# Group norm to the end in one block: memory normed once, its projections ahead of w_o and amid the conformer, norm gates and convolution taps between their tiles

## The reference, cut to what matters

```python
memn = rmsnorm(mem, mem_norm_g)                     # 256 memory tokens, the same in both layers
# layer 0: RWKV time mix. y is the scan's output, bonus and g come from the same inputs
m = jnp.mean(y, axis=-1, keepdims=True)             # over the 64 channels of a head
var = jnp.mean(jnp.square(y - m), axis=-1, keepdims=True)
y = ((y - m) * lax.rsqrt(var + GN_EPS)).reshape(B, T, D) * ln_g + ln_b
out = ((y + bonus) * g) @ w_o                       # g = sigmoid(xg @ g1) @ g2
# layer 1: conformer convolution
u = h @ w_in + b_in
u = u[..., :D] * jax.nn.sigmoid(u[..., D:])
u = causal_dwconv(u, dw) + dw_b                     # 31 taps for each channel
out = jax.nn.silu(layernorm(u, ln_g, ln_b)) @ w_out + b_out
# both layers, after x = x + out
x = x + memory_cross_attention(rmsnorm(x, g_x), memn, w_q, w_kv, w_o)   # kv = memn @ w_kv
x = x + conv_ffn(rmsnorm(x, g_f), w_in, dw3, w_out)
```

## Time and profile before

| | |
|---|---|
| median of 3 runs | 2953.36 us |
| profiled execution, its own time | 2956.45 us |
| its span, first to last instruction | 2954.7 us |
| TensorE (PE) busy | 2668.1 us, 90% |
| VectorE (DVE) busy | 1157.0 us, 39% |
| ScalarE (ACT) busy | 960.7 us, 33% |
| GpSimd (POOL) busy | 1004.0 us, 34% |
| mean granted clock of TensorE | 0.925 of 2.4 GHz |
| DMA moved | 197.90 MB, mean 67 GB/s |
| `mem`, loaded twice | 1024 KB each |
| `raw`, a chunk | 512 KB each, 346 of them |

### The profile page before, as it was taken

The page is one execution under the profiler, slowest core; times in us unless marked ns, Lnnn a source line. Parts: engine busy times, 40 slices in busy tenths (PEclk is TensorE's granted clock), DMA queues, the critical chain, the costliest instruction groups (busy, mean ns, idle before and its releaser), DMA issues. The chain is left out here.

```text
span 2954.7 us, 33055 instructions
## 1 busy us (share of the span) xinstructions
PE 2668.1 (90%) x12266; PEld 2032.4 (69%) x12266; DVE 1157.0 (39%) x1998; ACT 960.7 (33%) x1655; POOL 1004.0 (34%) x606
## 2 busy tenths in 40 slices
PE   4997789999989988998689899999988879999997
PEld 3873457888846667776168688888863577788885
DVE  2002365303152664532330345345397413354362
ACT  3234564212245351222133332223431533322222
POOL 1420144444522322110046154434520352444343
PEclk9997779999999997887689999999999889999998
DMA  3320001232311110000024122322220231223231
GB/s 123 95 78 0 1 1 65 93 100 95 122 50 57 50 37 1 1 1 24 33 95 129 35 86 93 114 85 89 97 71 0 72 114 57 72 93 107 86 99 58
DMA packets 52249, 197.90 MB, mean 67 GB/s; under 512 B 6205, under 2 KB 6333, under 8 KB 51037
## 3 DMA queue, kind: packets, MB, share of 16 engines
q1 hardware_dynamic: 50864, 189.62, 19.6%
q10 hardware_dynamic: 1262, 6.64, 0.6%
HBM read 194.15 MB, written 2.10 MB: 66 GB/s over the span
## 5 line engine op out<-in xcount | busy, mean ns | idle before, releaser
L487 POOL TENSOR_TENSOR w_lo<-raw,w_hi 128x1024 fp32r<-128x1024 f32 x342 | 817.3, 2399 | 1276.5 <-ACT w_hi L460 1276.3
L366 PE MATMUL ps<-ahead_hi,w_hi 128*128 128x512 f32 x1216 | 477.0, 392 | 4.3 <-PEq L3042 3.2
L368 PE MATMUL ps<-ahead_hi,w_lo 128*128 128x512 f32 x1216 | 474.1, 390 | 0.0
L367 PE MATMUL ps<-ahead_lo,w_hi 128*128 128x512 f32 x1216 | 473.9, 390 | 0.0
L460 ACT ACTIVATE w_hi<-raw 128x1024 fp32r<-128x1024 f32 x342 | 353.0, 1050 | 234.1 <-PE ps L356 94.4
L366 PEld LDWEIGHTS ps<-ahead_hi,w_hi 128*128 128x128 f32 x1216 | 228.8, 188 | 54.6 <-issue 5.2
L367 PEld LDWEIGHTS ps<-ahead_lo,w_hi 128*128 128x128 f32 x1216 | 228.8, 188 | 48.7 <-issue 1.4
L368 PEld LDWEIGHTS ps<-ahead_hi,w_lo 128*128 128x128 f32 x1216 | 228.7, 188 | 47.8
L600 DVE TENSOR_TENSOR x_stream<-x_stream,ps 128x512 f32<-128x512 f32 x80 | 54.9, 686 | 462.2 <-PE ps L368 257.9
L354 PE MATMUL ps<-ffn_a_hi,w_hi 128*128 128x512 f32 x352 | 139.5, 396 | 2.5 <-DVE ffn_a_lo L2984 2.5
L356 PE MATMUL ps<-ffn_a_hi,w_lo 128*128 128x512 f32 x352 | 139.1, 395 | 0.0
(11 more groups left out here) (424 smaller groups left out, 4926.9 us busy)
## 6 DMA issues: line engine op xcount, KB each, us to landing
raw<-in_wall SPq DMA_DIRECT2D x346, 512.0 KB, 3.4
x_stream<-in_x SPq DMA_DIRECT2D x1, 2048.0 KB, 9.1
cw<-in_cmp_w SPq DMA_DIRECT2D x1, 2048.0 KB, 7.5
mem<-in_mem ACTq DMA_DIRECT2D x2, 1024.0 KB, 5.8
out_y<-x_stream SPq DMA_DIRECT2D x1, 2048.0 KB, 6.3
dist<-in_consts ACTq DMA_DIRECT2D x1, 1748.5 KB, 7.1
lora_a<-in_lora_a ACTq DMA_DIRECT2D x1, 1152.0 KB
gwb<-in_lora_b SPq DMA_DIRECT2D x1, 1024.0 KB
```

The lines of the kernel that those rows point to most:

```text
L366: pe.matmul(out, hi, src.hi[:, t, 0:width], start=first, stop=False)
L367: pe.matmul(out, hi, src.lo[:, t, 0:width], start=False, stop=False)
L368: return pe.matmul(out, lo, src.hi[:, t, 0:width], start=False, stop=last)
L487: e.tensor_tensor(self.w.lo[:, s, :], self.raw[:, s, :], as_float(self.w.hi[:, s, :]), ALU.subtract).then_inc(lo_r.sem, 1)
```

## The change: what it does, and the diff

- Everything from the group norm to the last FFN is one block (`run(k, *stages)`). The ring is opened inside it: SP loads the memory first (1 MB), `gpick`, two chunks, `gwb`, and four more chunks. `open_ring`, `norm_memory`, the transposes and `pad` are no blocks any more.
- `GroupNorm` replaces `group_norm_and_gate` and `norm_memory`: the memory's squares lie on ACT between the group norm's, its sum on TensorE behind the fifth variance matmul, its scaling and split (`ms`) on DVE before the group norm's reciprocal. The memory is normed once; `ms` is kept for layer 1.
- w_kv of layer 0 stands before w_o in the stream. Its 16 tiles start when `ms` comes; gates 2 to 7 and the 8 spreads lie behind its tiles 1 to 8 (`fill`), DVE does its scale, bonus, gate and split meanwhile. The keys are evicted straight into `km`. The transposes of the values come behind w_o's first tile.
- `Conformer` replaces three classes: 7 taps a tile on TensorE (before 10), all 24 others on DVE, accumulating in the same bank. TensorE's taps lie behind tiles 3, 4, 6, 8, 12, 13 of the input product and tiles 2, 3 of w_kv; DVE's come in steps of 22 behind each pair of evictions from tile 5 on, the last 60 at the head of w_kv. w_kv of layer 1 comes between the conformer's input product and w_out; the layer norm's sums lie behind its tiles 6, 7, 11 (mean) and 13, 14 (variance); root, SiLU and split come at its end.
- The queries' eviction is unrolled; the FFN's memset moves onto POOL's queue; buffers lie elsewhere.

```diff
-PE_TAPS = 10
-EARLY_TAPS = 12
+PE_TAPS = 7
...
+class GroupNorm:
+    def sync(self, sp):
+        sp.dma_start(self.mem[:, :, :], a["mem"]).then_inc(ml.sem, 16)
+        sp.dma_start(self.picks[:, :], a["consts"][:, CST["pick"]:N_CONST]).then_inc(ld.sem, 16)
+        for n in range(2):
+            sp.dma_start(k.raw[:, n, :], k.wall[k.first + n]).then_inc(self.slots[n].sem, 16)
+        sp.dma_start(self.wb[:, :, :], a["lora_b"][:, 2:4, :]).then_inc(ld.sem, 16)
+        for n in range(2, k.lead):
...
+        mean(0)
+        mean(1)
+        for m in range(KD):
+            variance(m)                     # variance(0) waits for ld(32): picks and wb
+            if m + 2 < KD:
+                mean(m + 2)
+            if m == 4:
+                for n in range(KD):
+                    pe.wait_ge(squared.sem, squared(n + 1))
+                    mm = pe.matmul(k.ps[:, 4, 0:MEM], k.ones[:, :], self.sqm[:, n, :], start=(n == 0), stop=(n == KD - 1))
+                mm.then_inc(summed.sem, 1)
+        self.gate(pe, 0)
+        self.gate(pe, 1)
+        pe.wait_ge(rt.sem, rt(1))
+
+    def fill(self, pe, t):                  # behind tile t of w_kv
+        if 2 <= t < KD:
+            self.gate(pe, t)                # from t = 3 on waits for nd(t - 2)
+        if t == 1:
+            pe.wait_ge(iv.sem, iv(1))
+        if 1 <= t <= KD:
+            if t >= 2:
+                pe.wait_ge(n1.sem, n1(t - 1))
+            c = CST["spread"] - CST["pick"] + (t - 1) * P
+            pe.matmul(k.ps[:, 4, :], self.picks[0:rows, c:c + P], self.rtt[0:rows, 1, :], start=True, stop=True
+                      ).then_inc(sp_r.sem, 1)
...
+        for m in range(KD):                 # DVE, during w_kv
+            v.wait_ge(sp_r.sem, sp_r(m + 1))
+            v.scalar_tensor_tensor(y[:, m, :], y[:, m, :], k.vec("ln_g", m), k.ps[:, 4, :], ALU.mult, ALU.mult
+                                   ).then_inc(n1.sem, 1)
+            if m:
+                rest(m - 1)
+            shift(m)
+            gated(m)
+        rest(KD - 1)
...
+class Conformer:
+    PAIR_OPS = 2 * (TAPS - PE_TAPS)
+        step, n = 22, self.PAIR_OPS         # DVE, behind the eviction of pair f
+        if f == 2:
+            self.taps_vector(v, 0, 0, step)
+        elif f == 3:
+            self.taps_vector(v, 0, step, 2 * step)
...
+    def taps_tensor(self, pe, m):
+        pe.wait_ge(self.free.sem, self.free(2 * m + 2 + RING))
+        pe.wait_ge(self.dg.sem, self.dg(PE_TAPS * (m + 1)))
+        if m >= 4:
+            pe.wait_ge(self.kept.sem, self.kept(m - 3))
+        for t in range(PE_TAPS):
+            mm = pe.matmul(k.ps[:, m % 4, :], self.diag[:, m % 4, t, :], self.u[:, m, t:t + T], start=(t == 0),
+                           stop=(t == PE_TAPS - 1))
+    def inputs_tensor(self, pe, t):
+        for m in {3: (0,), 4: (1,), 6: (2,), 8: (3,), 12: (4,), 13: (5,)}.get(t, ()):
+            self.taps_tensor(pe, m)
+    def memory_tensor(self, pe, t):
+        if t in (2, 3):
+            self.taps_tensor(pe, 4 + t)
+        for m in {6: (0, 1, 2), 7: (3, 4, 5), 11: (6, 7)}.get(t, ()):
+            self.mean_tensor(pe, m)         # waits for kept(max(m, 4) + 1)
+        for m in {13: (0, 1, 2, 3), 14: (4, 5, 6, 7)}.get(t, ()):
+            self.variance_tensor(pe, m)
+    def memory_scalar(self, act, i, j):     # behind tile m of w_kv; keep: ACT copies a pair of sums out of PSUM
+        self.keys.taken(act, 4, m)
+        if m in (2, 5, 10):
+            self.keep(act, {2: 1, 5: 2, 10: 3}[m])
...
+    kv = Linear(k, 2 * KD, KD, ms, act=keys_scalar, width=MEM, ready=gn.fed, fill=gn.fill, unroll=True)
+    out = residual(k, KD, z, tmp, gain="xattn0", ready=gn.handed, prev=0, fill=keys.turn, early=keys.turned)
+    stages = [gn, kv, out]
     for layer in range(2):
-        km, vt = memory_keys(k, mem, room)
-        pad()
...
+        stages += [q, attention, os_, *ffn]
+        conformer = Conformer(k, at, top, ffn[-1].handed, KD)
+        kv = conformer.memory(again, ms)
+        out = residual(k, KD, conformer.out, tmp, bias="cb_out", gain="xattn1", ready=conformer.handed, prev=2 * KD,
+                       fill=again.turn, early=again.turned)
+        stages += [conformer.linear, kv, out]
+    run(k, *stages)
```

More of the change, by code:

```diff
@@ L2380, in vector @@
             some(p, 5)
[L2383 to L2426, removed]
-            pe.wait_ge(iv.sem, iv(1))
[L2428 to L2491, removed]
@@ L2577, in __init__, with queries @@
         k.advance(8, "pv_done", "mixer_out_hi", "mixer_out")
-    def queries(self):
+    def queries(self, ready):
         k, q_ = self.k, self.q
@@ L2590, in queries @@
         self.taken = free
-        return Linear(k, KD, KD, k.ahead, vector=vector, norm=True, bank=4)
+        return Linear(k, KD, KD, k.ahead, vector=vector, norm=True, bank=4, unroll=True, ready=ready, prev=KD)
     def sync(self, sp):
@@ L2766, in tap, with memory @@
+    def memory(self, keys, ms):
+        self.keys = keys
+        return Linear(self.k, 2 * KD, KD, ms, act=self.memory_scalar, vector=self.memory_vector, fill=self.memory_tensor,
+                      width=MEM, bank=4, prev=0, unroll=True)
     def tap(self, m, t):
@@ new lines, in taps_vector @@
+    def taps_vector(self, v, pair, first, last):
+        k, base = self.k, pair * self.PAIR_OPS
+        for n in range(first, last):
+            m, t = 2 * pair + n % 2, PE_TAPS + n // 2
+            bank = k.ps[:, m % 4, :]
+            if n < 2:
+                v.wait_ge(self.summed.sem, self.summed(m + 1))
+            else:
+                v.wait_ge(self.added.sem, self.added(base + n - 1))
+            v.scalar_tensor_tensor(bank, self.u[:, m, t:t + T], self.tap(m, t), bank, ALU.mult, ALU.add
+                                   ).then_inc(self.added.sem, 1)
@@ new lines, in second_block @@
+    ring = at(96)
+    k.raw, k.w = ring.tile("raw", RING, 1024), ring.split("w", RING, 1024)
+    k.lead, k.first, k.limit = RING + AHEAD, k.chunk, k.n_chunks
+    room = Arena(k, low + 148 * 1024)
+    k.ahead = Arena(k, top).split("ahead", KD, T)
+    small = at(24)
+    tmp = Scratch(small.tile("sqr", 2, T), small.tile("x_gained", 2, T))
+    ms, km, vt = at(32).split("ms", KD, MEM), at(48).tile("km", KD, MEM), at(56).tile("vt", 2, D)
+    turned = Arena(k, top + 24 * 1024).tile("kv_turned", KD, MEM)
```

553 lines of the change are left out of this document (286 added, 267 removed).

## The result

| | before | changed |
|---|---|---|
| median | 2956.45 us (4 runs, 2951.26 to 2962.57) | 2835.36 us (4 runs, 2822.86 to 2836.18) |
| profiled execution, its span | 2956.45, 2954.7 us | 2836.18, 2834.2 us |
| mean granted clock | 0.925 | 0.940 |

The ratio is 0.9577, with a 95% interval of 0.9557 to 0.9596: faster by 4.2%. The forecast was 2836 us, for a profiled execution 2839.

What follows compares the result with a forecast made beforehand. TensorE, busy 90% of the span, bounds the kernel, losing time idle or at low clock. 2956.45 less 61.0 (layer 0) and 59.4 (conformer) plus 3 gives 2839 profiled, 2836 us median; range 2824 to 2850, 8 in 10 2812 to 2874.

Steps and rivals of the forecast that it cites:

- loads to the first variance: Layer 0's start: `gwb` waits behind the memory and two chunks, 3.73 MB at 290 GB/s, 12.9 us, hidden by nothing.
- means, variances, memory's sum: Layer 0's group norm: means and variances 16.0 us as before, plus 3.6 for the memory's sum, 19.6 us.
- rounds and last taps of DVE: Conformer: DVE's rounds of evictions and 22 taps take 104.8 us, its last 60 taps with waiting 41.7.
- rival (e): Better: loads 10 us not 12.9, memory's sum hidden, spreads 0.9, no switch cost, no DVE wait: 2823 us; 12%.
- 31 us: Layer 0, 1419 to 1469: gates and spreads cost 31 us less than the former 50, part of the 61.0 gain.
- 3 us added for switches: Whole kernel: some thirty changes between kinds of matmul and waits behind them add 3 us.
- The rule weighed: Skill's rule that GpSimd contends with VectorE instructions having two SBUF inputs: 16 bonus and split instructions beside w_kv held.
- rival (a): POOL holds DVE: 16 instructions × 2.2 us in layer 0's w_kv, conformer taps at 0.747: 2861 us; 14%.
- signs of being wrong: DVE idle inside the taps, its splits over 1 us, clock near 0.5 over 20 us, or TensorE newly awaiting chunks.
- (b): Spreads of 16 rows keep the array at 1.2 GHz through layer 0's w_kv tiles 1 to 8: 2879 us; 7%.
- (c): Conformer: TensorE's pauses let the clock fall, 3052 us, slower; decides from 120 us of full-clock work at half; 2%.
- (d): Conformer: TensorE's order stalls DVE, so w_kv hides nothing; 41 us return, 2877 us; 5%.

Runs made afterwards that it cites:

- e5: Changed kernel with two of the three products left out in tiles 0 to 11 of layer 1's w_kv: 2826.8 us (one run).
- e2: Changed kernel with eight conformer taps a tile on TensorE instead of seven: 2837.61 us, ratio 0.9597.
- e4: Changed kernel with the loads' old order, earlier TensorE taps of tiles 6 and 7, and eight taps a tile on TensorE: 2816.77 us, ratio 0.9543.
- e4b: Changed kernel with the loads' old order and earlier TensorE taps of tiles 6 and 7, still seven taps a tile: 2828.23 us, ratio 0.9549.

## Why the prediction was right, step by step

All lengths in us; predicted, then read from the changed kernel's trace.

| step | predicted | measured |
|---|---|---|
| loads to the first variance | 12.9 | 11.8 |
| means, variances, memory's sum | 19.6 | 20.0 |
| to the end of w_kv's first tile | 9.8 | 9.2 |
| rest of w_kv with gates and spreads | 61.9 | 63.5 |
| w_o and transposes | 47.4 | 46.0 |
| queries, layer 0 | 44.4 | 44.4 |
| conformer to the sixth input tile | 45.9 | 46.1 |
| rounds and last taps of DVE | 146.5 | 147.2 |
| behind the last tap | 22.6 | 22.7 |
| to w_out's first tile | 18.9 | 18.7 |
| transposes, seven tiles, queries | 85.5 | 84.8 |
| sum | 515.4 | 514.5 |

**Layer 0.** The mechanism was right throughout: clock, order, and no engine but TensorE as the pace of w_kv. The 290 GB/s for the loads were too low: the stretch moved 361 GB/s, which goes the way of rival (e) (1.1 of its 2.9 us). The bytes were too few as well: the profile's KB are 1024 bytes, so the 3.73 MB are 3.82. The memory's sum took 3.62 us against 3.6. A whole round of w_kv took 5.83 us against 5.9, but by sizes that cancelled: the tile 2.97 (2.72), the gate 1.91 (2.11), the spread 0.95 (1.06). The prediction's "31 us" for gates and spreads doesn't follow from these prices, by which six gates and eight spreads are 21.1 us for the former 50, so 28.9; it isn't a term of the sum. In w_kv they took 19.3 us, 31 less. Before, TensorE was busy in 33 of the 50, so some 17 of the 31 are idle time and most of the rest is the clock.

**Two sizes that cancelled.** In w_kv's last tiles the evictions of ACT are 2.88 us apart, not 2.72:

```profile
1489.35 0.39 ACT L2587 ACTIVATE kv_turned<-ps 128x256 f32<-128x256 f32 x1 [1.55 <-PE ps L367]
...
1492.23 0.39 ACT L2587 ACTIVATE kv_turned<-ps 128x256 f32<-128x256 f32 x1 [1.55 <-PE ps L367]
```

That is 1.1 us over the seven tiles in layer 0. Against it a 512-column tile of w_o takes 5.44 us and not 5.60, 1.3 us over its eight and as much in w_out. I had taken both durations from the kernel before as fixed by shape; neither is, by 3 to 6%.

**How much of the hit is luck.** The 3 us added for switches between kinds of matmul found no row, beyond the 0.09 us by which a tile between gates is longer: without them the forecast for the profiled execution would have been 2836.05, and 2836.18 was measured. Two things outside the mechanism cancel in this: a start 3.2 us later, and 2.4 us that the unchanged stretches gave. For the median the prediction took off 3.1 us, as the profile before lay that much above the median of three runs (with a fourth the median is the profile's own 2956.45); this time it was 0.8. So the 3 us that were not there and the 2.3 us too many cancel too, and a median of 2835.36 beside 2836 is closer than the sum deserves. What the sum got right is the two gains, 62.0 and 59.3 beside 61.0 and 59.4.

**The conformer.** DVE sets the pace: 22 taps in 14.57 us (predicted 14.6), a round 17.3 us (17.6: two evictions took 1.29 us, not 1.47). What this gave back went into DVE's last wait, 3.70 us, not 1.9. TensorE's waits were 5.6 us behind tile 12 (7 predicted), 2.7 before w_kv (5) and 3.7 before the last means (5), and e5 shows that work taken off TensorE there mostly makes them longer. DVE then waited 3.80 us for the last means.

The prediction read the earlier trace rows as the taps of the two engines taking turns. They did not: TensorE's 70.9 us were unbroken, with DVE's taps beside them, and it was DVE that waited, 17.2 us. The forecast doesn't rest on this, since its rounds are summed from DVE's instructions and the products beside them.

**The rule weighed, and rival (a).** The hold exists, but it has no price here. DVE's timeline, then POOL's, in w_kv of layer 0:

```profile
1445.03 2.27 DVE L2562 TENSOR_TENSOR z_lo<-RA,z_hi 128x512 fp32r<-128x512 f32 x1
...
1450.20 0.75 DVE L2566 SCALAR_TENSOR_TENSOR RA<-RA,vecs,ps 128x512 f32<-128x512 f32 x1 [1.51 <-PE ps L2473]
1450.87 2.46 DVE L2562 TENSOR_TENSOR z_lo<-RA,z_hi 128x512 fp32r<-128x512 f32 x1
...
1462.53 2.85 DVE L2562 TENSOR_TENSOR z_lo<-RA,z_hi 128x512 fp32r<-128x512 f32 x1
```

```profile
1444.35 2.40 POOL L486 TENSOR_TENSOR w_lo<-raw,w_hi 128x1024 fp32r<-128x1024 f32 x1 [2.96 <-ACT w_hi L459]
1450.37 2.41 POOL L486 TENSOR_TENSOR w_lo<-raw,w_hi 128x1024 fp32r<-128x1024 f32 x1 [3.62 <-ACT w_hi L459]
...
1462.43 2.40 POOL L486 TENSOR_TENSOR w_lo<-raw,w_hi 128x1024 fp32r<-128x1024 f32 x1 [3.62 <-ACT w_hi L459]
```

Each `z_lo` that starts behind POOL's split ends 0.55 us after it: 1447.30 behind 1446.75, 1465.38 behind 1464.83. The later DVE starts, the shorter it lasts. This is not a shared rate but a wait for the other to end. One instruction a round is caught, 2.3 to 2.9 us for 0.7, not the two that rival (a) priced, and DVE still waits 0.9 to 1.7 us for TensorE's next spread (1.51 in the rows above). A DVE split over 1 us was one of the prediction's signs of being wrong; it came, and the slack beside TensorE swallowed it. My reading of the 44 unheld splits of the FFN as evidence against was wrong: they never meet POOL. In the changed kernel such a split runs from 1750.02 to 1750.71, and POOL's next chunk starts at 1751.02; the distance is 0.30 us for all 44, and in the kernel before as well. Nor was the memory's split held once: in the kernel before four of its 16 were (1.42 and 2.59 us in either layer), each ending 0.28 us behind POOL's. An instruction that isn't held says something only if the other engine is at work at that moment.

The Trainium skill says (SBUF — State Buffer, "Who interferes with whom") that the pair is an exclusive lock held for a whole instruction, and that a DVE instruction with at most one SBUF input, outside the 2-port perf modes, stays clear of it. This trace agrees on both: the ends above, and DVE's 22 taps in 14.57 us (`conv_u` in SBUF, the sum in PSUM), which rival (a) had feared at 0.747 each: 88 of the 192 taps overlap a split of POOL's, and none lasts longer than 0.756 us.

**The other rivals.** (b): the clock fell nowhere in w_kv (1.00), though the spreads use 16 rows. (c): 0.96, 0.97, 0.92 and 0.91 in the windows in which TensorE waits; its pauses are 5.6 us at most up to w_out and 8.9 before it, and the 120 us at half that would decide are not there. (d): refuted by e5. (e): in part (1.1 us of the loads, the 3 us of switches); the memory's sum didn't hide.

**What the prediction didn't see** is the slack left: 4.2 us in the order of the loads and 3.9 in the places of two tap groups, both of which it had described (12.9 us with nothing beside it; DVE's wait for tile 7's taps) and taken as given.

## What to carry to other kernels

Stages that take turns in short operations on several engines cost twice, in waiting and in the clock. Laid between dense products whose inputs are ready, the gates and spreads cost 19 us here instead of 50, and the products needn't be hidden themselves for that. The other half of layer 0's 62 us is mostly two stretches in which TensorE had next to no work (8.5 and 19.8 us) and that are gone. In the conformer the products themselves are hidden, beside an engine that is busy anyway. Where two engines run nearly level, moving work from one to the other (e2, 7.1 us lost) paid only together with the places at which they meet (e4 beside e4b, 1.7 us gained): first remove the wait, then shift the load. Judge an edit of a few microseconds by stage lengths inside the trace, when an unchanged part of the kernel scatters by more.
